# Weighted values with 128 stationary columns in two passes, halves added on the way out, divisions on GpSimd

## The reference, cut to what matters

```python
logits = jnp.where(mask, logits + decay, NEG)
p = jax.nn.softmax(logits, axis=-1).astype(v.dtype)
return jnp.einsum('bhqk,bkhd->bqhd', p, v)
```

## Time and profile before

| what | value |
|---|---|
| median of 3 runs | 1673.44 us (1670.68 to 1679.44) |
| the profiled execution | 1673.03 us, its span 1671.2 us |
| mean granted clock of TensorE | 0.974 of full speed |
| PE busy | 1584.1 us, 95% |
| DVE busy | 888.0 us, 53% |
| ACT busy | 629.0 us, 38% |
| POOL busy | 111.6 us, 7% |

### The profile page before, as it was taken

How to read it: one execution, slowest core, us unless ns; L and a number is a source line. 1 busy time by engine, 2 the same in 40 slices (tenths; PEclk the granted TensorE clock), 3 DMA queues, 4 the chain that set the end, 5 groups by cost and what they waited for, 6 DMA issues and landing times.

```text
span 1671.2 us, 28828 instructions
## 1 busy us (share of the span) xinstructions
PE 1584.1 (95%) x11210; PEld 1496.5 (90%) x11210; DVE 888.0 (53%) x1578; ACT 629.0 (38%) x1132; POOL 111.6 (7%) x153
## 2 busy tenths in 40 slices
PE   4999979998999999999999897999899999999997
PEld 3787768887999999999999686888899999999997
DVE  4232048896345545555465246889535555555544
ACT  3313148875322222222233435887533222222213
POOL 2110011110200000000000001111020000000000
PEclk8999979999999999999999998999999999999998
DMA  7245332213212222122120536221322232231101
GB/s 258 92 133 160 122 97 58 57 29 101 76 62 90 77 74 100 53 98 75 47 70 10 190 135 205 64 63 32 102 76 76 76 100 72 78 100 58 67 0 57
DMA packets 119309, 145.99 MB, mean 87 GB/s; under 512 B 17633, under 2 KB 95521, under 8 KB 119249
## 3 DMA queue, kind: packets, MB, share of 16 engines
q1 hardware_dynamic: 119248, 145.16, 26.9%
HBM read 120.54 MB, written 24.60 MB: 87 GB/s over the span
## 4 chain that ended last, share of the span: by engine, by line
PE 58%; issue 29%; DVE 7%; ACT 4%; DMA 1%; POOL 1%; SPq 0%; DVEq 0%; POOLq 0%; ACTq 0%
PE ps L1373 50%; DVE nmx L1077 2%; DVE ptl L1102 2%; ACT pth L792 2%; PE ps L1538 2%; PE ps L1582 1%; PE ps L1584 1%; PE ps L1583 1%; PE ps L1553 1%; DVE ol L1113 1%; POOL sacc L613 1%; DVE prob L1091 1%; ACT oh L803 0%; ACT prob L782 0%; ACT wh L698 0%
## 5 line engine op out<-in xcount | busy, mean ns | idle before, releaser
L1225 DVE TENSOR_TENSOR xT<-xT,ps 128x592 f32<-128x592 f32 (+1 forms) x256 | 195.3, 763 | 189.4 <-PE ps L1373 188.1
L698 ACT ACTIVATE wh<-raw 128x2048 fp32r<-128x2048 f32 (+1 forms) x90 | 167.1, 1872 | 235.0 <-PE ps L1373 234.9
L977 DVE TENSOR_TENSOR wl<-raw,wh 128x2048 fp32r<-128x2048 f32 (+1 forms) x90 | 200.8, 2243 | 76.3 <-ACT wh L698 76.2
L1373 PE MATMUL ps<-hh,wh 128*128 128x296 f32 (+1 forms) x1024 | 221.9, 298 | 0.0
L1373 PE MATMUL ps<-xgh,wh 128*128 128x296 f32 (+1 forms) x1024 | 221.9, 298 | 0.0
L1373 PE MATMUL ps<-xgl,wh 128*128 128x296 f32 (+1 forms) x1024 | 221.2, 297 | 0.0
L1373 PE MATMUL ps<-hl,wh 128*128 128x296 f32 (+1 forms) x1024 | 220.8, 297 | 0.0
L1373 PE MATMUL ps<-xgh,wl 128*128 128x296 f32 (+1 forms) x1024 | 220.3, 296 | 0.0
L1373 PE MATMUL ps<-hh,wl 128*128 128x296 f32 (+1 forms) x1024 | 220.0, 296 | 0.0
L863 ACT ACTIVATE hh<-hw 128x592 fp32r<-128x592 f32 (+1 forms) x64 | 44.3, 693 | 351.2 <-DVE hw L1209 351.2
L1373 PEld LDWEIGHTS ps<-hl,wh 128*128 128x128 f32 x1024 | 166.1, 188 | 0.0
(11 more groups left out here) (196 smaller groups left out, 2721.0 us busy)
## 6 DMA issues: line engine op xcount, KB each, us to landing
raw<-in_w_up SPq DMA_DIRECT2D x32, 1024.0 KB, 5.5
raw<-in_w_down SPq DMA_DIRECT2D x32, 1024.0 KB, 4.9
raw<-in_w_in_a SPq DMA_DIRECT2D x12, 1024.0 KB, 7.3
kv_mla<-stn SPq DMA_DIRECT2D x24, 256.0 KB, 2.1
raw<-in_w_o_a SPq DMA_DIRECT2D x4, 1024.0 KB, 7.5
natk<-kv_mla SPq DMA_DIRECT2D x8, 512.0 KB, 4.2
raw<-in_w_o_b SPq DMA_DIRECT2D x4, 1024.0 KB, 11.0
q_mla<-stn SPq DMA_DIRECT2D x16, 192.0 KB, 1.9
```

Of the source, the lines that this page charges most:

```text
L698: s.activation(wh[:, j % 4, 0:r * c], raw[:, j % 4, 0:r * c], ACT.Copy).then_inc(hi_done, 1)
L977: v.tensor_tensor(wl[:, j % 4, 0:r * c], raw[:, j % 4, 0:r * c], wh[:, j % 4, 0:r * c].bitcast(F32), ALU.subtract).then_inc(lo_done, 1)
L1225: v.tensor_tensor(a, a, two_banks(2 + m % 2, n), ALU.add).then_inc(x_ready if last else acc_done, 1)
L1373: return te.matmul(out, a, b, start=start, stop=stop)
```

## The change

The values' halves lie side by side in one tile `vhl`: for each key tile and head, 64 high and 64 low columns. The first pass takes all 128 as stationary columns, so that high by high lands in PSUM partitions 0 to 63 and low by high in 64 to 127. The second pass multiplies the high values with the low probabilities into partitions 0 to 63. VectorE adds the lower partitions to `ol` in a second instruction, which waits for the first. All five divisions of a head move to GpSimd, as a `tensor_tensor` with the reciprocal broadcast. `split_v` is cut in three parts that are placed between the divisions of every second head from head 4 on. The waits of `p_turn` now all use `p_ready`, and `p3_ready` is gone.

```diff
@@ GpSimd @@
+            def normalise(layer, h, c, u):
+                n = unit_keys(u)[1]
+                rows = P if u < NT else TX
+                off = P_OFF[u] + (64 if u < NT else 0)
+                pool.wait_ge(recip_done, h * 5 + (5 * HEADS * layer + u + 1))
+                g.tensor_tensor(prob[0:rows, c, off:off + n], prob[0:rows, c, off:off + n],
+                                rs[0:rows, u:u + 1].to_broadcast([rows, n]), ALU.mult).then_inc(p_ready, 1)
...
+            def attention(layer):
+                def head(h, c):
+                    for u in range(5):
+                        normalise(layer, h, c, u)
+                def head_and_v(h, c, j, slot, turn):
+                    for u in range(3):
+                        normalise(layer, h, c, u)
+                        split_v(layer, j, slot, turn, u, True)
+                    normalise(layer, h, c, 3)
+                    normalise(layer, h, c, 4)
+                for j in range(2):
+                    for part in range(3):
+                        split_v(layer, j, j, 0, part)
+                for h in range(4):
+                    head(h, h % 2)
+                with pool.Fori(0, PAIRS // 2 - 1) as i:
+                    head_and_v(4 * i + 4, 0, 2 * i + 2, 0, i + 1)
+                    head(4 * i + 5, 1)
+                    head_and_v(4 * i + 6, 0, 2 * i + 3, 1, i + 1)
+                    head(4 * i + 7, 1)
@@ ScalarE @@
-                        if u == 0 and not first:
-                            scale3(h - 1, 1 - c)
@@ VectorE, out @@
                     v.tensor_tensor(ol[rows, pair, :], pf[0:HD, 3072:3072 + T], oh[rows, pair, :].bitcast(F32),
-                                    ALU.subtract).then_inc(o_lo, 1)
+                                    ALU.subtract).then_inc(o_part, 1)
+                    dve.wait_ge(o_part, head + (H0 + 1))
+                    v.tensor_tensor(ol[rows, pair, :], pf[HD:P, 3072:3072 + T], ol[rows, pair, :].bitcast(F32),
+                                    ALU.add).then_inc(o_lo, 1)
@@ VectorE, step @@
-                        scale(h - 1, 1 - c, 4)
-                    scale(h, c, 0)
-                    scale(h, c, 1)
-                    scale(h, c, 2)
@@ TensorE, p_turn @@
-                    if u == 3:
-                        pe.wait_ge(p3_ready, h + H0)
-                    else:
-                        pe.wait_ge(p_ready, h * 4 + (4 * H0 + [-3, -2, -1, 0, 0][u]))
+                    pe.wait_ge(p_ready, h * 5 + (U0 + u - 4))
@@ TensorE, weighted_v, parts 0 to 2; part 3 likewise @@
-                            te.matmul(out, vh[0:rows, vs, t, d], pr_h, start=(b == 0), stop=False, skip_group_check=True)
-                            te.matmul(out, vh[0:rows, vs, t, d], pr_l, start=False, stop=False, skip_group_check=True)
-                            te.matmul(out, vl[0:rows, vs, t, d], pr_h, start=False, stop=(b == 1), skip_group_check=True)
+                            te.matmul(pf[:, cols], vhl[0:rows, vs, t, p, :, :].rearrange("p s d -> p (s d)"), pr_h,
+                                      start=(b == 0), stop=False, skip_group_check=True)
+                            te.matmul(pf[0:HD, cols], vhl[0:rows, vs, t, p, 0, :], pr_l, start=False, stop=(b == 1),
+                                      skip_group_check=True)
```

More of the change, by code:

```diff
@@ L116, in build @@
         natv0 = at("natv0", [P, 7, P], F32, R_G + 12736)
-        vh = at("vh", [P, 2, 7, P], F32R, R_G + 23552)
-        vl = at("vl", [P, 2, 7, P], F32R, R_G + 23552 + 7168)
+        vhl = at("vhl", [P, 2, 7, 2, 2, HD], F32R, R_G + 23552)
         yT = at("yT", [P, KD, T1], F32, R_G)
@@ L637, in _, with split_v @@
                               tab[0:TILE_ROWS[t], t, 8 * hf:8 * hf + 8, :]).then_inc(aug_done, 1)
-            def split_v(layer, j, slot, turn, after_av=False):
-                if layer == 0:
-                    pool.wait_ge(nat_v, j * 64 + 64)
-                else:
-                    pool.wait_ge(nat_qk[slot], turn * 80 + (80 + 40 * PAIRS))
-                if after_av:
-                    pool.wait_ge(av_done, j * 2 + (HEADS * layer - 2))
+            def normalise(layer, h, c, u):
[5 more added lines that the diff above has]
+                                rs[0:rows, u:u + 1].to_broadcast([rows, n]), ALU.mult).then_inc(p_ready, 1)
+            def split_v(layer, j, slot, turn, part, after_av=False):
+                if part == 0:
+                    if layer == 0:
+                        pool.wait_ge(nat_v, j * 64 + 64)
+                    else:
+                        pool.wait_ge(nat_qk[slot], turn * 80 + (80 + 40 * PAIRS))
+                    if after_av:
+                        pool.wait_ge(av_done, j * 2 + (HEADS * layer - 2))
                 views = []
@@ L653, in split_v @@
                     views.append((src, slice(0, rows), slice(t0, t1)))
[L654 to L669, removed]
+                if part == 0:
+                    src, r, t = views[0]
+                    g.tensor_tensor(vhl[r, slot, NT, :, 0, :], src.rearrange("p t h d -> p (t h) d"),
+                                    ones[r, :].rearrange("p (h d) -> p h d", h=2), ALU.mult).then_inc(v_hi, 1)
+                    for src, r, t in views[1:]:
+                        g.tensor_copy(vhl[r, slot, t, :, 0, :], src).then_inc(v_hi, 1)
+                    pool.wait_ge(v_hi, j * 3 + 3 + 3 * PAIRS * layer)
+                    return
@@ new lines, in split_v @@
+                for src, r, t in (views[0:1] + views[2:3] if part == 1 else views[1:2]):
+                    i = g.tensor_tensor(vhl[r, slot, t, :, 1, :], src, vhl[r, slot, t, :, 0, :].bitcast(F32), ALU.subtract)
+                if part == 2:
+                    i.then_inc(v_split, 1)
+            def attention(layer):
[18 more added lines that the diff above has]
+                    head(4 * i + 7, 1)
@@ L671, in _ @@
+            attention(0)
             sum_squares(1)
@@ L676, in _ @@
                 g.tensor_tensor(rc[:, i, :], ss[:, i, :], mhalf[:], ALU.pow).then_inc(zr_ready, 1)
[L677 to L681, removed]
+            attention(1)
             sum_squares(3)
@@ L804, in out @@
                                  ACT.Copy).then_inc(o_hi, 1)
[L806 to L810, removed]
                 def step(h, c, pair, first=False, last=False):
@@ L1083, in recip @@
                     v.reciprocal(rs[0:rows, u:u + 1], sm[0:rows, u:u + 1]).then_inc(recip_done, 1)
[L1085 to L1090, removed]
-                    v.tensor_scalar(prob[0:rows, c, off:off + n], prob[0:rows, c, off:off + n], rs[0:rows, u:u + 1],
-                                    None, ALU.mult).then_inc(p_ready, 1)
                 def group(h, q, what):
@@ L1176, in attention @@
                 recip(HEADS - 1, 4)
-                scale(HEADS - 1, 1, 4)
                 for k in range(1, 6):
```

17 lines of the change are left out of this document (6 added, 11 removed).

## The result

The change made the kernel slower: 1690.33 us (median of 6 runs, 1686.22 to 1692.68) against 1677.28 (6 runs, 1670.68 to 1679.44), a ratio of 1.0085 with the 95% interval 1.0064 to 1.0105. The forecast was 1676, its range ended at 1689. The profiled execution took 1690.06 us.

The account below looks back on a forecast made before the run. It took a chain of two stretches, PE's and then ACT's and DVE's, as the bound. Steps +2.2 and layer 1's start +1.5 made +3.7 on the profiled 1673.03; it said +3, 1676 us, range 1662 to 1689.

Parts of the forecast that it names:

- The steady step: Each attention step of one head, 10.1 us: -0.50 - 0.27 + 0.85 = +0.08 us, bounds -0.12 to +0.27.
- PE's saving: Fewer passes on PE between p_turn 0 and p_turn 1: 0.41 to 0.53 us shorter a step, taken as 0.50.
- Unit 1's division: The only division taken to be on the chain, in DVE's run before the split of group 3: 0.27 us saved a step.
- The second instruction of `out`: Added in DVE's unbroken run, with its wait for the first: +0.85 us a step, bounds 0.68 and about 0.95.
- count of 28 steps: The step's +0.08 us holds in 28 of 32 steps, as `out` starts in the third: +2.2 us, bounds -3.4 to +7.6.
- The start: Layer 1's start: POOL divides the first head only after splitting pair 1, so PE waits; +1.5 us, bounds 0.5 to 3.
- The layer ends: At each layer's end the second instruction of `out` (+0.8) and the fewer passes (-0.9) cancel.
- The clock: PE's lower clock was counted only at layer 1's start, up to 1 us more there; nothing elsewhere.
- Faster: DVE's chain has give and absorbs the 0.85 us: 1653 if all, 1665 if half; chance 0.2.
- POOL too slow: Broadcast multiplication or waits make POOL's divisions late; at double price 1702 us; chance 0.12.
- DVE blocked by POOL: DVE instructions are held while POOL works; one 1 us hold in each of 28 steps gives 1704; chance 0.08.
- Slower by the waits: The new self-wait on DVE costs over 0.3 us more than priced: +8 to +14 us, 1683 to 1687; chance 0.1.

## Why the prediction was wrong

**The steady step: right in its parts, one term too small.** PE's saving was put at 0.50 us and is 0.48. Unit 1's division was put at 0.27 and is 0.28, by the kernel with the divisions alone. The second instruction of `out` was put at 0.85 with 0.95 as the upper bound, and is 0.94 by taking it away. The pair's 1.48 us to the reciprocal was right (1.49), and its 0.80 is the term that the working could read from rows. What it lacked is the 0.11 us behind the reciprocal: the split of the keys reads PSUM from partition 0 after an instruction that read it from partition 64, and loses its overlap. The wait, to which the working gave the lost overlap ahead of the second instruction, is free only because the partitions hold that instruction anyway. So the step grew by 0.20 and not by 0.08. The working's count of 28 steps was right, and they are +6.1 instead of +2.2, inside its bound of +7.6.

**The start: the mechanism was right, its size partly luck.** It was put at +1.5 with bounds of 0.5 and 3, and p_turn 0 is 1.95 us later, on the only wait of PE for POOL in the trace. The first step then takes 9.61 instead of 11.04 us. That can't be counted on: two later kernels with the same delay took 11.37 for it, as their clock came back 9.6 us behind p_turn 0 and here 5.6.

**The layer ends: the cancellation was right at full clock.** The working had "the second instruction of `out` (+0.8) and the fewer passes (-0.9) cancel". The wait for `ol` behind the first pair of `out` is 0.9 us longer in the second layer, and by the kernel that kept its clock there the passes save about 1.1. The layer ends are 4.5 us longer all the same, because the clock fell.

**The clock: the step that failed.** The working put nothing for TensorE's clock outside the first layer's start and took all other stretches at full speed, without a reason. Where it put +0.85 us on DVE and -0.50 on PE, it said who sets the pace but not what PE then does: it stands idle for 0.7 to 1.0 us in each step and for up to 1.96 us at the layer ends. The runs show some 10 us of lower clock in its place, 5.3 in three steps and about 4.9 in the layer ends. This missing term took the result out of the range; the other errors lie within the bounds. Together: 3.7 forecast, +3.9 for the steps, +0.4 for the start less 1.8 in the first steps, -0.2 for the layer ends at full clock, +5.3 and +4.9 for the lower clock, gives 16.2, where 16.0 were found.

**The rivals.** "Faster" is refuted, as DVE's run has no give: all of the second instruction, and 0.2 us more, shows in the step. "POOL too slow" and "DVE blocked by POOL" are refuted by the kernel with the divisions alone, which is faster. POOL's divisions by shape (groups by form, both layers) were cheaper than priced:

```profile
L643 POOL TENSOR_TENSOR prob<-prob,rs 128x528 f32<-128x528 f32 x32 | 34.1, 1066 | 0.0
...
L643 POOL TENSOR_TENSOR prob<-prob,rs 128x400 f32<-128x400 f32 x32 | 27.3, 852 | 47.0 <-DVE rs L1099 47.0
```

The five of a head sum to 3.73 us, not 4.5: 1.67 ns for each further column, where the subtraction of two full inputs takes 2.13. That one also writes another format, and no run separates this from the broadcast. The rule of "GPSIMD Engine Reference", "When to use GPSIMD", in the Trainium skill, that elementwise work is slower there, holds (852 ns for 400 columns, DVE's mean was 398). It did not decide the time: the work stood on no chain but at the start. "Slower by the waits" came nearest to the size (+8 to +14), but its cause is refuted by the run without the wait.

**What stays open.** What decides which steps fall to the lower clock: from the second to the fourteenth none in the kernels where PE's waits are short or filled, three in the changed one, but six in the one whose steps are 0.14 us shorter. A last step fell with its wait filled, and one layer end kept its clock behind a wait of 1.83 us. With that, whether the 2 us of the start show in the time, and 3 of the 11 us that the divisions alone gain.

## What to carry to other kernels

When a change takes work from one engine and puts less than that on another, look for the exact place where the second has no pause: 0.7 us added inside DVE's unbroken run cost 0.94 a step, while 0.66 us put where ACT waited anyway cost 0.07 (a step of 9.41 against 9.34), and turned a ratio of 1.009 into 0.989. Count the neighbours of a new VectorE instruction too, above all the next reader of PSUM when it begins in other partitions. Then work out how long TensorE stands idle in each step and look whether its granted clock holds there; it is better to remove such a wait (1657.5 us) than to fill it (1689.3).

## What the runs showed of the hardware

The granted clock of TensorE can fall to the lower level in the middle of a stage, with pauses of 0.7 to 1.0 and of some 0.45 us in a step of 10.7 us. With passes added in the longer pause it stayed at 1.00 in all steps but the first and the last of a layer, and 35 us were the difference. One kernel's executions differed along with it: 14 us between a mean clock of 0.968 and 0.960. A pass with 128 stationary columns is about as short as one with 64: ten passes took 1.11 us, where 0.118 for each with 256 moving columns and half of that for 128 would give 1.06. POOL's multiplication with a broadcast operand took a fifth less per column than its subtraction of two full inputs. And a VectorE instruction that read PSUM from partition 64 behind one that read it from 0 started 0.1 us later than one that read from 0 again, and so did the next one that read from 0.
